# Memory values computed after the attention instead of inside it, and 110 instead of 106 tokens through the row path, in a float32 transformer kernel on one core

## The reference

```python
# layer 1: h = rmsnorm(x); projections of h; two attention branches
ya, yb = moba_attention(...), nsa_attention(...)          # 8 heads each, over 256 tokens
g = sigmoid(mgate.reshape(B, S, 2, D) + b_merge)          # 2 x 1024 gate columns of h @ w_in
x = x + (g[:, :, 0] * (ya @ w_up_a) + g[:, :, 1] * (yb @ w_up_b)) @ w_out
# 16384 experts, one neuron each; 8 heads pick 16 experts for every token
a = einsum('cd,chkd->chk', x2, expert_u[ec]);  w = gelu(a) * gates
x = x + einsum('chk,chkd->cd', w, expert_v[ec])           # 128 experts for each token
# two more layers: mixer, cross attention over 256 memory tokens, convolutional FFN,
# each followed by layer_norm(x, g, b) with the residual
k, v = split(mem @ xa_wkv[layer])                         # depends on mem alone
```

## Time and profile before

| what | value |
|---|---|
| time of the kernel before, median of 3 runs (lowest, highest) | 1756.58 us (1754.37, 1758.73) |
| time of the profiled execution | 1756.63 us |
| its span, first to last instruction | 1754.8 us |
| granted TensorE clock, mean over the span | 0.996 |
| read from HBM, written | 432.69 MB, 5.24 MB |

### The profile page before, as it was taken

How to read it: one execution, slowest core, us unless ns; L and a number is a source line. 1 busy time by engine, 2 the same in 40 slices (tenths; PEclk the granted TensorE clock), 3 DMA queues, 4 the chain that set the end, 5 groups by cost and what they waited for, 6 DMA issues and landing times.

```text
span 1754.8 us, 29426 instructions
## 1 busy us (share of the span) xinstructions
PE 1719.8 (98%) x11729; PEld 1467.0 (84%) x11729; DVE 1116.6 (64%) x2415; ACT 240.8 (14%) x600; POOL 297.4 (17%) x282
## 2 busy tenths in 40 slices
PE   8999999999999899999999999999999999999996
PEld 7887576987999899999999858699946979699942
DVE  4653534898656988899433542379965762379964
ACT  1016511111423111000000011011100001011100
POOL 0010000244333444444322200000000000000000
PEclk9999999999999999999999999999999999999998
DMA  7543243699999999999999745354454535344451
GB/s 279 186 155 142 73 147 116 238 323 392 413 416 416 409 411 395 401 414 415 417 417 418 289 202 189 116 217 170 168 178 154 175 137 191 112 167 170 170 176 48
DMA packets 76608, 439.62 MB, mean 251 GB/s; under 512 B 8566, under 2 KB 8656, under 8 KB 37840
## 3 DMA queue, kind: packets, MB, share of 16 engines
q1 hardware_dynamic: 42624, 305.15, 46.1%
q0 software_dynamic: 32592, 125.92, 18.3%
q10 hardware_dynamic: 1280, 6.96, 1.0%
HBM read 432.69 MB, written 5.24 MB: 250 GB/s over the span
## 4 chain that ended last, share of the span: by engine, by line
PE 81%; DMA 10%; DVE 8%; issue 1%; ACT 0%; POOL 0%; SPq 0%; POOLq 0%; DVEq 0%
PE ps L1144 16%; PE ps L930 14%; PE ps L543 10%; DMA arena<-u_rows,sparse_pairs 8%; PE ps L587 7%; PE ps L922 7%; PE ps L1182 4%; PE ps L626 3%; PE ps L501 3%; DVE arena L1919 2%; PE ps L783 2%; PE ps L832 2%; PE ps L796 2%; DMA ring<-stream 1%; PE ps L943 1%
## 5 line engine op out<-in xcount | busy, mean ns | idle before, releaser
L922 PE MATMUL ps<-xT,ring 128*128 128x150 f32 x2048 | 267.8, 293 | 0.0
L930 PE MATMUL ps<-arena,ring 128*128 128x150 f32 (+1 forms) x2048 | 266.3, 292 | 0.8 <-DMA ring<-stream 0.8
L922 PEld LDWEIGHTS ps<-xT,ring 128*128 128x128 f32 x2048 | 263.8, 191 | 0.1
L930 PEld LDWEIGHTS ps<-arena,ring 128*128 128x128 f32 x2048 | 262.2, 190 | 1.0 <-issue 1.0
L2040 DVE SCALAR_TENSOR_TENSOR arena<-arena,sparse_dots 128x1024 f32<-128x1024 f32 x105 | 134.7, 1283 | 74.7 <-DMA arena<-v_rows,sparse_pairs 69.4
L543 PE MATMUL ps<-ring,arena 128*128 128x512 f32 x416 | 181.4, 592 | 0.4 <-ACT arena L1494 0.4
L1919 DVE CUSTOM_DVE_ANT_0 arena<-arena 128x1024 f32<-128x1024 f32 x107 | 128.1, 1223 | 67.1 <-DMA arena<-u_rows,sparse_pairs 66.5
L2508 POOL DMA_INDIRECT arena<-v_rows,sparse_pairs x107 | 132.5, 1239 | 221.7 <-DVE arena L2040 176.0
L2471 POOL TENSOR_SCALAR stat<-stat 128x1 f32<-128x1 f32 (+2 forms) x23 | 4.4, 191 | 905.6 <-DVE stat L2212 705.7
L2508 POOL DMA_INDIRECT arena<-u_rows,sparse_pairs x107 | 128.7, 1203 | 171.0 <-DVE sparse_dots L1919 147.4
L543 PEld LDWEIGHTS ps<-ring,arena 128*128 128x128 f32 x416 | 78.0, 190 | 92.9 <-issue 92.3
(11 more groups left out here) (342 smaller groups left out, 2210.7 us busy)
## 6 DMA issues: line engine op xcount, KB each, us to landing
ring<-stream SPq DMA_DIRECT2D x288, 1024.0 KB, 7.6
arena<-second_params POOLq DMA_DIRECT2D x6, 1024.0 KB, 5.3
arena<-kv_scratch POOLq DMA_DIRECT2D x2, 2048.0 KB, 14.8
kv_scratch<-arena ACTq DMA_DIRECT2D x2, 1024.0 KB, 11.2
arena<-held_params ACTq DMA_DIRECT2D x1, 2048.0 KB, 16.6
arena<-u_rows,sparse_pairs POOLq DMA_INDIRECT x107, 14.5
arena<-v_rows,sparse_pairs POOLq DMA_INDIRECT x107, 12.0
arena<-second_params POOLq DMA_DIRECT2D x1, 1536.0 KB, 6.3
```

Source lines behind the costliest of these rows:

```text
L922: ins = pe.matmul(ps[:, o % 2, 0:DENSE], w[:, (o % 2) * D + k * P:(o % 2) * D + (k + 1) * P], xT[:, k, 0:DENSE], start=(k == 0), stop=(k = ...
L930: ins = pe.matmul(ps[:, 4 + k // 2, c:c + DENSE], w[:, (o % 2) * D + k * P:(o % 2) * D + (k + 1) * P], H[:, n, :], start=first and k % 2 = ...
```

## The change

The change has nine parts.

1. `v0` leaves the attention and is computed after the peer queries, ahead of `k1` (`memory_values`). Its slots move in `SECTIONS` with it. ACT copies it from two banks and writes it to DRAM, where POOL did that before.
2. The merge gates are now the fill of all 16 units, 4 products of 256 columns for each. DVE adds the bias after every fourth unit (`raw_gates`), and ACT applies one sigmoid to all of them after the loop.
3. The heads of the first five head groups are turned between the compression slots 2 and 3, the rest after them.
4. Four more tokens go by rows, each on 32 partitions. This makes 4 more `u` fetches and 4 more `v` fetches (111 each, 222 turns), 8 small transfers of pair numbers, one more copy of token rows (8 transposes on PE ahead of `k0b`), and 8 more products when the sums are folded. `DENSE` is 146. The number of groups stays 19.
5. The turns in DVE's list shift by 8: 78 before `sel16`, 84 before the second one-hots, 124 and 172 at the ends of the two `mixed`. The stretch behind them is as long as before.
6. The weights of the first 64 rows are taken at group 5 instead of group 7 (`WEIGH_GROUP`).
7. `layer_norm` has two passes instead of three. The first, (x - mean) * g, no longer waits for the inverse root.
8. In the last normalisation, PE's last 512 columns go as two pieces of 256.
9. The first slot and the memory are loaded as a quarter and three quarters instead of two halves.

The diff, cut to its core:

```diff
 SPARSE_B = 42
-SETS_B = P // SPARSE_B
-SPARSE = SPARSE_A + SPARSE_B
+SPARSE_C = 4
+SETS_B, SETS_C = P // SPARSE_B, P // SPARSE_C
+SPARSE = SPARSE_A + SPARSE_B + SPARSE_C
 DENSE = T - SPARSE
...
-CHUNKS = PAIRS_HALF + PAIRS_B
+FIRST_C = PAIRS_HALF + PAIRS_B
+PAIRS_C = P // SETS_C
+CHUNKS = FIRST_C + PAIRS_C
...
-DOTS_FIRST = 70
-DOTS_TURN = 74
-TURNS_UP = 116
-TURNS_DOWN = 164
+DOTS_FIRST = 78
+DOTS_TURN = 82
+TURNS_UP = 124
+TURNS_DOWN = 172
 GATES_AT = 22
 WEIGH_AT = 8
-WEIGH_GROUP = 7
+WEIGH_GROUP = 5
 LAST_ADDS = 14
...
 SECTIONS = [("k0a", K0_FIRST), ("proj", 10), ("bc", 1), ("mgate_a", 4), ("cmp", 4), ("mgate_b", 4),
-            ("v0", 4), ("merge", 4), ("w_out", 4), ("peer_q", 8), ("k1", 4), ("v1", 4),
+            ("merge", 4), ("w_out", 4), ("peer_q", 8), ("v0", 4), ("k1", 4), ("v1", 4),
             ("k0b", 4 - K0_FIRST),
             ("peer_u", HALF_BLOCKS), ("peer_v", HALF_BLOCKS),
...
-            half = SLOT // 2
+            half = SLOT // 4
...
-                    for hf in range(2):
+                    for bank, c, w, started in ((6, 0, 512, True), (3, 512, 256, False), (7, 768, 256, False)):
+                        if c == 512:
+                            pe.wait_ge(moments_ready, 13)
                         for s in range(4):
                             for k in range(2):
-                                ins = pe.matmul(ps[:, bank0 + 2 + hf, :], act_of(2 * s + k, 1),
-                                                held[s][:, k * D + hf * 512:k * D + (hf + 1) * 512],
-                                                start=(bank0 + 2 + hf in start and s == 0 and k == 0),
+                                ins = pe.matmul(ps[:, bank, c % 512 % w:c % 512 % w + w], act_of(2 * s + k, 1),
+                                                held[s][:, k * D + c:k * D + c + w],
+                                                start=(not started and s == 0 and k == 0),
                                                 stop=(s == 3 and k == 1))
-                            if hf:
+                            if c == 768:
                                 ins.then_inc(slot_done, 1)
-                        if hf == 0:
+                        if c < 768:
                             ins.then_inc(tile_psum, 1)
 
             def y2_tile(k, i):
...
+            def turn_heads(us):
+                for u in us:
+                    pe.wait_ge(qk_ready, u // 2 + 1)
+                    if u >= 4:
+                        pe.wait_ge(qkT_ready, u - 3)
+                    for j in range(2):
+                        for i in range(TT):
+                            c = (2 * u + j) * P
+                            ins = pe.transpose(ps[:, 4 + u % 4, (2 * j + i) * P:(2 * j + i + 1) * P],
+                                               qkv[:, i, c:c + P], ident)
+                    ins.then_inc(qkT_psum, 1)
...
+                if kv == 1:
+                    pe.wait_ge(proj_added, 5)
+                    turn_heads(range(5))
...
+                s, t, kh = n // 4, n // 2 % 2, n % 2
+                if t == 0 and kh == 0:
+                    if s:
+                        pe.wait_ge(gate_raw, s)
+                    fill_slots["gate"] = slot("mgate_b", s)
+                w = fill_slots["gate"]
+                for k in range(4 * kh, 4 * kh + 4):
+                    ins = pe.matmul(ps[:, 6, t * T:(t + 1) * T], w[:, k * 2 * P + t * P:k * 2 * P + (t + 1) * P],
+                                    xT[:, k, :], start=(k == 0), stop=(k == KT - 1))
...
+            def memory_values(name, before):
+
+                for half in range(2):
+                    v_slots = [slot(name, 2 * half + kh) for kh in range(2)]
+                    for i in range(TT):
+                        if 2 * half + i or before > K0_FIRST:
+                            pe.wait_ge(xkv_ready, before + 2 * half + i - 1)
+                        for kh in range(2):
+                            for k in range(4):
+                                ins = pe.matmul(ps[:, 4 + i, :], memT[:, 4 * kh + k, i * P:(i + 1) * P],
+                                                v_slots[kh][:, k * 512:(k + 1) * 512],
+                                                start=(kh == 0 and k == 0), stop=(kh == 1 and k == 3))
+                            if i == 1:
+                                ins.then_inc(slot_done, 1)
+                        if i == 0:
+                            ins.then_inc(v_psum, 1)
...
+            memory_values("v0", K0_FIRST)
             for c in range(4):
-                if c >= 2:
-                    pe.wait_ge(xkv_ready, KV_EARLY + c - 1)
+                pe.wait_ge(xkv_ready, V0_DONE + c - 1)
                 feature_major(slot("k1", c), 4 + c % 2, memT).then_inc(slot_done, 1)
...
+            memory_values("v1", K1_DONE)
+            pe.wait_ge(x_last_wide, 1)
+            pe.wait_ge(xres_T_ready, 4)
+            for k in range(KT):
+                ins = pe.transpose(ps[:, 2 + k // 4, (k % 4) * P:(k % 4 + 1) * P], x_wide_c[:, k], ident)
+            ins.then_inc(x_last_psum, 1)
...
+                for part, (name, n) in enumerate((("fold", SPARSE_A), ("fold_b", SPARSE_B), ("fold_last", SPARSE_C))):
+                    c = (k % 2) * T + (T - SPARSE_A, DENSE + SPARSE_C, DENSE)[part]
+                    ins = pe.matmul(ps[:, 4 + k // 2, c:c + n], row_sums[part][:, k * P:(k + 1) * P], sm(name),
...
+            act.wait_ge(gate_raw, 4)
+            act.activation(gT_b, gT_b, ACT.Sigmoid).then_inc(mgate_ready, 1)
...
+            copy_values("v0", 0, v0_stage)
+            act.wait_ge(xkv_ready, V0_DONE)
+            act.dma_start(kv_scratch[0][:, KT * T:], v0_stage.rearrange("p i n -> p (i n)")).then_inc(v0_spilled, 16)
+            gate_exponentials(0)
...
+            def raw_gates(s):
+
+                dve.wait_ge(slot_done, START["mgate_b"] + s + 1)
+                for t in range(2):
+                    n = 2 * (4 + s) + t
+                    a = SMALL["b_merge"][0] + n
+                    ins = dve.tensor_scalar(gT[:, n, :], ps[:, 6, t * T:(t + 1) * T], small[:, a:a + 1], None, ALU.add)
+                ins.then_inc(gate_raw, 1)
...
+                if u < NU and u % 4 == 3:
+                    raw_gates(u // 4)
...
+                    a, width = 64 + 12 * i, 12
                     if n == 5 and i == 1:
-                        for hf in range(2):
-                            if hf == 0:
-                                dve.wait_ge(tile_psum, n + 3)
+                        a, width = 64, 24
+                        for q in range(4):
+                            if q < 3:
+                                dve.wait_ge(tile_psum, n + 3 + q // 2)
                             else:
                                 dve.wait_ge(slot_done, done)
-                            v = xres[:, i, 512 * hf:512 * (hf + 1)]
-                            link(dve.tensor_tensor(v, v, ps[:, 4 + 2 * i + hf, :], ALU.add))
-                            ins = dve.bn_stats(stat[:, a + 6 * hf:a + 6 * hf + 6], v)
+                            v = xres[:, i, 256 * q:256 * (q + 1)]
+                            of = ps[:, (6, 6, 3, 7)[q], (0, 256, 0, 0)[q]:(256, 512, 256, 256)[q]]
+                            link(dve.tensor_tensor(v, v, of, ALU.add))
+                            ins = dve.bn_stats(stat[:, a + 6 * q:a + 6 * q + 6], v)
                     else:
                         for hf in range(2):
...
+                    pieces = (slice(0, 512), slice(512, D)) if n == 5 else (slice(0, D),)
+                    for c in pieces:
+                        v = xres[:, i, c]
+                        ins = dve.scalar_tensor_tensor(v, v, stat[:, 50 + 2 * i:51 + 2 * i], ln_p[:, n, 0, c],
+                                                       ALU.subtract, ALU.mult)
+                    link(ins)
                     dve.wait_ge(ln_rstd, 2 * n + 3 + i)
-                    for c in ((slice(0, 512), slice(512, D)) if n == 5 else (slice(0, D),)):
+                    for c in pieces:
                         v = xres[:, i, c]
-                        link(dve.tensor_scalar(v, v, stat[:, 50 + 2 * i:51 + 2 * i], stat[:, 54 + i:55 + i],
-                                               ALU.subtract, ALU.mult))
-                        link(dve.tensor_tensor(v, v, ln_p[:, n, 0, c], ALU.mult))
-                        dve.tensor_tensor(v, v, ln_p[:, n, 1, c], ALU.add).then_inc(x_ready, 1)
+                        dve.scalar_tensor_tensor(v, v, stat[:, 54 + i:55 + i], ln_p[:, n, 1, c],
+                                                 ALU.mult, ALU.add).then_inc(x_ready, 1)
                     if n < 5:
                         turned(n + 3, i)
 
...
+                    for t in range(SPARSE_C):
+                        for n in range(2):
+                            pool.dma_start(pairs[SETS_C * t:SETS_C * (t + 1), n, FIRST_C:],
+                                           pairs_out_b[c_first + t:c_first + t + 1, n, 0:P]
```

(8 more changed lines are left out.)

176 lines of the change are left out of this document (65 added, 111 removed).

## The result

The changed kernel takes 1764.74 us (median of 8 runs, 1761.38 to 1766.42), the kernel before 1757.49 (8 runs, 1754.06 to 1760.07). The ratio is 1.0039, with a 95% interval of 1.0028 to 1.0051: slower by some 7 us. The forecast was 1753.0, its range ended at 1764. So the sign was wrong, and the time lies just outside.

What follows compares the result with a forecast made beforehand. PE, busy 98%, was taken to bound the kernel. From 1756.63 us, -2.1 - 18.6 + 10.1 + 8 + 1 + 1.8 - 1.1 - 2.7 = -3.6 gave 1753.0 us, range 1743 to 1764.

Steps and rivals of the forecast that it cites:

- The compression: Between compression slots 2 and 3: twenty transposes cover PE's 2.4 us wait for a slot, -2.1 us.
- the attention: MoBA units 3.43 us each, -14; NSA units about 6.2 us, 3.6 kept in eight; with 1 us for ACT, -18.6.
- the return of `v0`: Ahead of `k1`: the value products that left the attention come back on PE's list, +27.6 us.
- the loss of the normalisations' waits: In the normalisations: PE's waits for DVE go with fewer passes, -1.1 us.
- the rows come late and PE waits for `residual(0)`: At the end of the experts: row transfers arrive late and PE waits there, +8 us, ends 0 and +16.
- rival A: In the experts: rows are not late and PE's list alone sets the time, 1744 us; chance 0.27.
- five rows at 1.6 us each: Before `residual(0)`: five rows taken as short, each costing 1.6 us, giving the +8 us wait.
- the wait at the second gates: In the experts: PE's 4.56 us wait for DVE's one-hots and the slow records behind it go, -5.9 us.
- the four columns: In the experts: 4096 records have 146 columns for 150, at 0.76 ns a column, -12.5 us.
- The forecast's sum of bytes: In the experts: 533.5 us at 412 GB/s carries 219.8 MB, so 201 of 208 rows fit, seven short.
- Rival B: In the experts: the stream is late, not the rows, and 9.4 MB cost 22.9 us, 1756.8 us; chance 0.15.
- The +1 for the weights at group 5: In the experts: weights at group 5 ask for gelu results that ACT has barely made, +1 us (0 to 3).

Runs made afterwards that it cites:

- small edits: The kernel before with only compression order, normalisations, last pieces and quarter loads changed: 1751.80 us, ratio 0.9969.
- narrow columns alone: The changed kernel without its four more tokens by rows, with 146 columns anyway (experts of four tokens left out): 1751.31 us, ratio 0.9954 to the kernel before.
- 108 tokens with wide gate products: The changed kernel with two tokens in the fourth group, and its 32 branch-gate records widened from 24 to 128 columns: ratio 0.9980 to the kernel before.
- 106 tokens: The changed kernel with the fourth group of tokens taken out, 150 columns and the old turn numbers: 1754.91 us, ratio 0.9983 to the kernel before.
- 108: The changed kernel with two tokens instead of four in the fourth group, 148 columns: 1754.87 us, ratio 0.9981 to the kernel before.
- the ratios 0.9958 and 0.9920: To the kernel before: its version with compression, normalisation, last-piece and load edits plus 128-column branch gates; then also four turns fewer ahead of the one-hots (1744.77 us).

## Why the prediction was wrong

*Right.* The compression, the attention (3.4 and 6.2 us a unit), the return of `v0` and the loss of the normalisations' waits came within 1 us of the forecast. The mechanism that was new in it was right too: the rows come late and PE waits for `residual(0)`, 5.85 us where 8 was taken. With it rival A, which had no such wait, fell. The small edits measured alone gave 5.4 us.

*Right in size by luck: that wait.* The forecast took five rows at 1.6 us each. The rows came every 3.5 to 3.8 us to the last, so 5.85 us is between one and two rows. Two errors more or less cancel in that count: 3.5 rows fewer were done at the start (next paragraph), and PE's last sums came 543.1 us into the stage, not 533.5, which gave the rows 9.6 us more.

*The step that failed: the wait at the second gates "goes, with 4 to 11 us to spare".* It stayed, at 5.67 us, with 1.9 us of clock behind it: 7.6 us in the wrong column. Three numbers in the step were off. The row products of the changed kernel, up to the experts and then for 142.9 us:

```profile
270.00:437.40 167.40, 48.23 (x81) 1.00 0.79 297
437.40:580.30 142.90, 52.62 (x88) 1.00 1.02 410
```

That is 40.5 rows before the experts, not 44. In the longer memory stage rows do not come at the pace of 12 in 28 us. Over the second value product it is 21 records in 28.3 us, 10.5 rows, with the transfers full:

```profile
395.30:423.60 28.30, 12.22 (x21) 1.00 1.02 407
```

The slots of `v0` and its copy to DRAM are what was added to them there; that they took the rows' share was not tried by itself. The 43.5 rows that are left, at 3.3 us each, end 143 us into the stage, and not 133. Then DVE still makes the one-hots, from 579.80 to 582.89 us in its timeline: 3.1 us that the forecast left out. And PE arrives there after 139.9 us, and not 144: the forecast had counted from the end of the old wait, 575.38, and not from its start, 4.56 us earlier. So the spare time of 11 us is short by 10, 3 and 4 us. The rows and the one-hots together would have left a wait of 1 to 2 us; PE's arrival alone would have left none.

What a forecast without this error would have missed is less clear than the 7.6 us: with the long wait gone (row turns moved behind the gates) the kernel was only 2.6 us shorter, and short waits stood in its place.

*Mis-sized: the four columns.* 2.65 ns a record, so -10.9 and not -12.5. The forecast took 130.8 ns for a record of 150 columns from the groups; its own have 114.57/896 = 127.9, which would have given 2.5 ns.

*Mis-priced: what a faster PE does to the rows.* The forecast's sum of bytes had it (a shorter stage carries fewer rows), but it then took a late row at 1.6 us, as if the stream made room at the end, and in the step of the gates a fixed 3.3 us. Up to `residual(0)` a late row costs 3.5 to 3.8 us. The run with narrow columns alone shows the whole effect: 21 us of slack gone (14.4 and 6.9), 13 because PE had its last sums sooner (11 of them are the columns) and 8 because the last row came later.

The sum of bytes itself holds. With the 44 rows and the 133.7 MB of the forecast it gives 543 us for the stage, near the 541.5 that the forecast had (533.5 and the wait of 8). With what was measured, 208 - 40.5 rows of 0.529 MB, 135.0 MB of the stream and 3.1 MB of other queues, it gives 226.7 MB or 550 us at 412 GB/s, and the stage took 548.9. So the rows that were missing at the start stand behind most of the miss in the experts, in this view too.

So it is the rows that give way, at an unchanged total rate. The Trainium skill ("DMA: Bandwidth & Descriptors", section "Queues, rings and completion order") has the packet rotation between queues that would make this. The trace agrees: with both queues busy the rows get 141 of 412 GB/s, and when PE takes slots sooner the stream's bytes grow at the rows' cost (20.58 for 19.79 MB). Rival B, in which the stream pays, fell: PE waits 1.2 us for the ring.

*Missing: the clock.* Beside the one at the second gates there are three falls, with 1.7 us behind the narrow products, 2.05 behind the wait at the residual, and 1.5 behind the fold. They cover the 1.1 us at the start and the 3.2 behind the experts. The fold was 3.66 us of 64-column products, 32 records, and is now 5.51, 48 records, and the 64 records behind it took 8.93 us for 7.39. This goes with the longer fold over all profiles: behind 32 records the next 64 took 7.39 us in each of eight, behind 48 they took 8.65 to 9.95 in five of six and 7.39 in one (108 tokens with wide gate products). In two of the five PE had also stood 1.1 or 3.2 us in front of the fold. A fold of 48 wide records was not tried.

The end of the kernel gained 1.7 and not 2.7 us. From PE's last product to DVE's last pass it takes 4.17 us for 6.62, a gain of 2.45 that is close to the forecast. But from there to the end of the span, where the output leaves, it takes 8.99 us for 8.22. With the same edits that was 8.29 with 106 tokens and 8.65 with 108; no run shows why. The +1 for the weights at group 5 was not measured by itself either.

## What to carry to other kernels

Where two queues fill the transfer engines, a faster consumer of the one slows the other, so work that is shifted from the engine to the transfers is paid twice. Measure the slack at the point where both meet, and stop before it is used up (here between 108 and 110 tokens). A wait that is removed stays gone only if slack stands behind it: moving four or five turns gave 2.6 us without slack and, by the ratios 0.9958 and 0.9920, 6.7 with 14 us of it. Count arrival times from the start of a wait, not from its end, and add what the other engine still does behind the event that you count. Where all transfers are full, bytes over rate give the length of the stage, if the count of what is done at its start is right (550 us for 548.9 here, and 543 with a count that was 3.5 rows too high and a stream 1.3 MB too small).

## What the runs showed of the hardware

The granted clock fell while PE was busy all the time, behind 32 records of 24 columns: to 0.50 to 0.58 over the next four us in six of nine profiles, and never behind the same records with 128 columns. Behind 48 records of 64 columns the next 64 records took 8.65 to 9.95 us in five of six profiles, behind 32 such records 7.39 in each of eight. It also fell behind waits: the 64 records behind `residual(0)` took 9.0 to 9.4 us in the four profiles in which PE had stood 2.0 to 6.9 us there, and 7.38 in the ten with 0.61 us.

With two queues at a full DMA share the sum stayed at 416 GB/s over 80 us while 0.8 MB went from the one to the other, as PE took the stream's slots 2% faster.

An execution's time follows the mean clock: the kernel before ran from 1753.4 us at 0.997 to 1763.8 at 0.992. What else starts such a fall, and why only in some executions, stays open.
